# A feed-forward down projection computed with seven half-size products in place of eight

## The reference

```
FFN_HIDDEN = -(-8 * D_MODEL // (3 * 256)) * 256        # 2816

def swiglu(x, w_gate, w_up, w_down):
    return (jax.nn.silu(x @ w_gate) * (x @ w_up)) @ w_down

for l in range(DEPTH):                                  # DEPTH = 2
    mix = hybrid_mixer(x, ...)
    x = layer_norm(ALPHA * x + mix, ln1_g[l], ln1_b[l])
    ffn = swiglu(x, w_ffn_gate[l], w_ffn_up[l], w_ffn_down[l])
    x = layer_norm(ALPHA * x + ffn, ln2_g[l], ln2_b[l])
```

## Time and profile before

| | |
|---|---|
| median of three runs | 2691.89 us (2689.46 to 2693.79) |
| the profiled execution | 2692.8 us, span 2691.0 us |
| PE busy | 2336.5 us, 87% of the span |
| PE weight loads busy (beside PE) | 1520.1 us, 56% |
| DVE busy | 744.4 us, 28% |
| ACT busy | 369.2 us, 14% |
| mean granted clock of TensorE | 0.948 of 2.4 GHz |
| HBM traffic | 241 GB/s over the span |
| the down stage (L2028) in the two layers | 464.05 to 539.78 us and 1006.30 to 1082.03 us |

### The profile page before, as it was taken

One profiled execution on the slowest core, in us unless ns is written; L12 is line 12 of the kernel. 1 busy time (PEld: TensorE's weight loads), 2 busy tenths in 40 slices (PEclk: granted clock), 3 DMA queues, 4 the chain that ended last, 5 costly groups with the idle time before them and its releaser, 6 DMA issues.

```text
span 2691.0 us, 38118 instructions
## 1 busy us (share of the span) xinstructions
PE 2336.5 (87%) x16872; PEld 1520.1 (56%) x16872; DVE 744.4 (28%) x1501; ACT 369.2 (14%) x837; POOL 26.1 (1%) x48
## 2 busy tenths in 40 slices
PE   8999999989999999899989997888799876656564
PEld 6788688477886884445545555554454543323322
DVE  1201472022014730534443221222211441101111
ACT  1211000012210000225433000000102320000000
POOL 0000000000000000000000000000000000000000
PEclk9999999999999999999989999999999988878777
DMA  8443786453436873300044999999910078999996
GB/s 296 153 145 126 242 290 219 146 199 130 152 125 230 286 249 128 135 0 1 1 188 160 423 426 426 426 426 427 381 68 0 0 302 365 427 427 427 428 427 283
DMA packets 165415, 651.84 MB, mean 242 GB/s; under 512 B 7846, under 2 KB 55298, under 8 KB 140290
## 3 DMA queue, kind: packets, MB, share of 16 engines
q1 hardware_dynamic: 161680, 639.66, 61.1%
q0 software_dynamic: 3056, 8.79, 1.0%
q10 hardware_dynamic: 514, 0.94, 0.1%
HBM read 648.27 MB, written 1.08 MB: 241 GB/s over the span
## 4 chain that ended last, share of the span: by engine, by line
PE 55%; issue 28%; DMA 12%; DVE 3%; ACT 1%; DVEq 0%; POOL 0%; SPq 0%; ACTq 0%; POOLq 0%
PE psum L2012 11%; DMA ring<-in_moe_w_up 9%; PE psum L1856 8%; PE psum L1933 6%; PE psum L2028 5%; PE psum L464 4%; PE psum L661 4%; PE psum L1921 3%; PE psum L588 2%; PE psum L456 2%; DMA ring<-in_moe_w_gate 2%; PE psum L678 1%; PE psum L1834 1%; PE psum L1882 1%; DMA ring<-in_moe_w_down 1%
## 5 line engine op out<-in xcount | busy, mean ns | idle before, releaser
L661 PE MATMUL psum<-ring,arena 128*32 128x256 f32 x5952 | 390.9, 419 | 168.7 <-DMA ring<-in_moe_w_up 83.6
L661 PEld LDWEIGHTS psum<-ring,arena 128*32 128x32 f32 x5952 | 212.4, 119 | 343.1 <-issue 143.7
L2012 PE MATMUL psum<-ht,ring 128*128 128x256 f32 x1408 | 311.1, 382 | 2.1 <-ACT ht L2068 2.1
L2012 PEld LDWEIGHTS psum<-ht,ring 128*128 128x128 f32 x1408 | 267.4, 191 | 44.4 <-issue 9.1
L678 PE MATMUL psum<-ring,lnp 128*32 128x256 f32 x3072 | 194.5, 408 | 69.2 <-DMA ring<-in_moe_w_down 63.8
L464 PE MATMUL psum<-ring,ht 128*128 128x512 f32 x448 | 195.0, 594 | 0.0
L678 PEld LDWEIGHTS psum<-ring,lnp 128*32 128x32 f32 x3072 | 104.5, 116 | 158.5 <-DMA ring<-in_moe_w_down 50.6
L1419 DVE TENSOR_TENSOR arena<-psum,gb_moe 32x512 f32<-32x512 f32 (+1 forms) x128 | 70.9, 554 | 373.6 <-PE psum L678 372.3
L1933 PE MATMUL psum<-ht,ring 128*128 128x256 f32 x768 | 166.7, 380 | 0.0
L1933 PEld LDWEIGHTS psum<-ht,ring 128*128 128x128 f32 x768 | 146.3, 190 | 20.3 <-issue 1.0
L2028 PE MATMUL psum<-ring,arena 128*128 128x512 f32 x352 | 151.6, 593 | 1.9 <-DVE arena L2309 1.9
(11 more groups left out here) (350 smaller groups left out, 1933.5 us busy)
## 6 DMA issues: line engine op xcount, KB each, us to landing
ring<-in_moe_w_gate SPq DMA_DIRECT2D x64, 2048.0 KB
ring<-in_moe_w_down SPq DMA_DIRECT2D x64, 2048.0 KB
ring<-in_moe_w_up SPq DMA_DIRECT2D x60, 2048.0 KB
ring<-in_w_in SPq DMA_DIRECT2D x52, 1024.0 KB
ring<-in_ada_w SPq DMA_DIRECT2D x48, 1024.0 KB
ring<-in_w_ffn_gate SPq DMA_DIRECT2D x22, 1024.0 KB
ring<-in_w_ffn_up SPq DMA_DIRECT2D x22, 1024.0 KB
ring<-in_w_ffn_down SPq DMA_DIRECT2D x20, 1024.0 KB
```

Of the source, the lines that this page charges most:

```text
L661: last = mm(bank[32 * j:32 * j + 32, SPLIT * m:SPLIT * m + SPLIT], x_four[:, k, e % 4, SLOTS * m:SLOTS * m + SLOTS], row[:, SPLIT * j:SPLI ...
L2012: last = mm(bank[:, SEQ * u:SEQ * u + SEQ], slot[:, k, SEQ * u + P * h:SEQ * u + P * h + P], xT[:, k, :], start=k == 0, stop=k == KT - 1)
```

## The change

The products of each pair of hidden tiles are regrouped by Strassen's scheme (in the form with seven products). The 256 tokens are cut in two halves of 128, the 1024 columns in two of 512, and the 22 hidden tiles are taken in 11 pairs (`PAIRS`). A quarter of `hid` is then one tile of a pair for one half of the tokens, a quarter of the weights one tile of a pair for one half of the columns. For each pair PE now computes seven products of 128x128 with 128x512, in the order 1, 6, 5, 2, 3, 7, 4 (`SEVEN`), each product number having a bank of its own that accumulates over the 11 pairs.

- **Sums of `hid`** (`turned(a, b)`, DVE): four instructions for the pairs a to b-1. Pairs 0 to 7 are done in one go after p = 8 (four instructions of 128x1024), pair 8 after p = 9, pair 9 after p = 10, pair 10 after the four copies out of the bank `adaGT` (four instructions of 128x128 each). One of the four writes over a quarter of `hid`.
- **Sums of the weights** (`down_sums(d)`, DVE): four instructions for each down panel, 128x1024 for d = 0 to 4 and 128x512 for d = 5. One of them writes over a part of the ring slot, three go to one of three buffers. `down_sums(0)` comes at p = 8, after `turned(0, 8)`; the others come after the gate products. From d = 3 on each waits until PE has finished panel d-3.
- **PE** opens seven banks in place of four before the first product. It goes through panels 0 to 3 pair by pair, and releases each; for panels 4 and 5 (three pairs) it goes product by product, so that the seven banks are finished one after the other, three products apart. Panels 4 and 5 are both released at the end.
- **The tail**: ACT copies the banks of products 1 and 5 to SBUF; DVE combines the seven into the four quarters of `x` (`scaled`, `plus`), normalises t = 0 after product 3, and then adds products 7 and 4 and normalises t = 1. The order of the products in the tail is the same in both layers.
- The tile `gb_moe` of the second network is now a view of a new tile `spare` of the same size, which holds weight sums in the first. `DVE_LAYER`, the number of DVE's counted steps in the loop, goes from 36 to 62.

In the extracts of the instruction order below, `[waits ...]` names the semaphores an instruction waits for, and xN repeats it. L2012 of before is L2022 now, L2309 is L2373, L2319 is L2388, L2257 has become L2400 to L2419, and L2264 to L2274 are L2296 to L2306.

The core of the diff:

```diff
-DVE_LAYER = 36
+DVE_LAYER = 62
+PAIRS = FFN_TILES // 2
+SEVEN = (1, 6, 5, 2, 3, 7, 4)
...
-    layer += [EV] * 5 + [("dn", t, n) for t in range(TT) for n in range(2)]
+    layer += [EV] * 4 + [("dn", c) for c in SEVEN] + [R]
...
-                down = {(t, n): open_bank(pe, "layer", ("dn", t, n), l) for t in range(TT) for n in range(2)}
+                down = {c: open_bank(pe, "layer", ("dn", c), l) for c in SEVEN}
                 wait_emptied(pe, "layer", ("ff", FFN_TILES - 1), l)
-                for f in range(0, FFN_TILES, 4):
-                    slot = panel(l, D)
...
+                    a11, a12, a22 = hid[:, 2 * i, 0:P], hid[:, 2 * i + 1, 0:P], hid[:, 2 * i + 1, P:SEQ]
+                    s1, s2, s4 = (hid_sums[:, m, i, :] for m in range(3))
+                    s3 = hid[:, 2 * i, P:SEQ]
...
+                    return {1: (a11, b11), 2: (a12, b21), 3: (s4, b22), 4: (a22, t4), 5: (s1, t1), 6: (s2, t2),
+                            7: (s3, t3)}[c]
+                slots = [panel(l, D)]
+                pe.wait_ge(hid_sums_ready, l * 4 + 1)
+                for d in range(4):
+                    if d:
+                        slots.append(panel(l, D))
+                    pe.wait_ge(w_sums_ready, l * 6 + (d + 1))
+                    for i in (2 * d, 2 * d + 1):
+                        for c in SEVEN:
+                            left, right = factors(c, i, slots[d], w_sums[d % 3])
+                            last = mm(down[c], left, right, start=i == 0, stop=False)
+                    last.then_inc(pe_done, 1)
+                slots += [panel(l, D), panel(l, D)]
+                pe.wait_ge(hid_sums_ready, l * 4 + 4)
+                pe.wait_ge(w_sums_ready, l * 6 + 6)
+                for c in SEVEN:
+                    for i in range(8, PAIRS):
+                        left, right = factors(c, i, slots[i // 2], w_sums[i // 2 % 3])
+                        last = mm(down[c], left, right, start=False, stop=i == PAIRS - 1)
+                    last.then_inc(pe_done, 1)
...
+                for c, part in ((1, part_1), (5, part_5)):
+                    take(("dn", c), part, part=HALF)
                 root(1, 0)
...
+                def turned(a, b):
+                    for f in range(2 * a, 2 * b):
+                        wait_emptied(dve, "layer", ("ff", f), l)
+                    h4 = hid.rearrange("p (i c) n -> p i c n", c=2)[:, a:b]
+                    a11, a21, a12, a22 = (h4[:, :, c, P * r:P * r + P] for c in range(2) for r in range(2))
+                    s1, s2, s4 = (hid_sums[:, m, a:b, :] for m in range(3))
+                    step(TTo(s1, a21, a22, ALU.add))
+                    step(TTo(s2, s1, a11, ALU.subtract))
+                    TTo(a21, a11, a21, ALU.subtract)
+                    TTo(s4, a12, s2, ALU.subtract).then_inc(hid_sums_ready, 1)
+                def down_sums(d):
+                    n_panel = DOWN_PANEL + d
+                    dve.wait_ge(panel_in[n_panel % RING], l * (32 * LAYER_PANELS // RING) + 32 * (n_panel // RING + 1))
+                    if d >= 3:
+                        dve.wait_ge(pe_done, down_full(d - 3))
...
+                    TTo(t3, b22, b12, ALU.subtract)
+                    step(TTo(b12, b12, b11, ALU.subtract))
+                    step(TTo(t2, b22, b12, ALU.subtract))
+                    TTo(t4, b21, t2, ALU.subtract).then_inc(w_sums_ready, 1)
...
+                    if p == 8:
+                        turned(0, 8)
+                        down_sums(0)
+                    elif p > 8:
+                        turned(p - 1, p)
...
-                for t in range(TT):
-                    add_residual([("dn", t, n) for n in range(2)])
-                    layer_norm(1, t, ln2_loaded, x_ready)
+                turned(PAIRS - 1, PAIRS)
+                dve.wait_ge(pe_done, banks.full("layer", ("ff", FFN_TILES - 1), l))
+                down_sums(1)
+                dve.wait_ge(mods_saved, l * 64 + 64)
+                for d in range(2, 6):
+                    down_sums(d)
...
+                scaled(x00, part_1)
+                plus(part_12, part_1, 6)
+                scaled(x01, part_12)
+                wait_emptied(dve, "layer", ("dn", 5), l)
+                step(TTo(x01, x01, part_5, ALU.add))
+                scaled(x11, part_5)
+                plus(x00, x00, 2)
+                plus(x01, x01, 3)
+                layer_norm(1, 0, ln2_loaded, x_ready)
+                plus(part_all, part_12, 7)
+                scaled(x10, part_all)
+                step(TTo(x11, x11, part_all, ALU.add))
+                plus(x10, x10, 4)
+                layer_norm(1, 1, ln2_loaded, x_ready)
```

More of the change, by code:

```diff
@@ L1588, in program @@
     LAYER_PANELS = banks.stage_panels["layer"][1]
-    ADA_PANEL = 22
+    ADA_PANEL, DOWN_PANEL = 22, 40
     assert LAYER_PANELS % RING == 0
@@ L1610, in program @@
         lnp = sb("lnp", [P, 2, D])
+        spare = sb("spare", [P, 2 * D])
         const = sb("const", [P, 904])
@@ L1643, in program @@
         ada_rows = view(arena[:, 6656:6912], 2, P)
+        hid_sums = view(arena[:, 9984:14208], 3, PAIRS, P)
+        w_sums = [[view(spare[:, 0:1024], 2, HALF), view(spare[:, 1024:2048], 2, HALF), view(arena[:, 14208:15232], 2, HALF)],
+                  [view(ht[:, 1024 * m:1024 * m + 1024], 2, HALF) for m in range(3)],
+                  [view(arena[:, 6912 + 1024 * m:7936 + 1024 * m], 2, HALF) for m in range(3)]]
+        part_1, part_12 = arena[:, 5632:6144], arena[:, 6144:6656]
+        part_5, part_all = ht[:, 3072:3584], ht[:, 3584:4096]
         xT = view(ht[:, 0:2048], KT, SEQ)
@@ L2019, in _, with factors @@
                         transposes("layer", ("adaGT",), [ada_g[:, P * j:P * j + P] for j in range(2)], l)
[L2020 removed]
+                down = {c: open_bank(pe, "layer", ("dn", c), l) for c in SEVEN}
                 wait_emptied(pe, "layer", ("ff", FFN_TILES - 1), l)
[L2022 to L2033 removed]
+                def factors(c, i, slot, sums):
+                    a11, a12, a22 = hid[:, 2 * i, 0:P], hid[:, 2 * i + 1, 0:P], hid[:, 2 * i + 1, P:SEQ]
+                    s1, s2, s4 = (hid_sums[:, m, i, :] for m in range(3))
+                    s3 = hid[:, 2 * i, P:SEQ]
+                    r = i % 2
+                    b11, t1 = slot[:, 2 * r, 0:HALF], slot[:, 2 * r, HALF:D]
+                    b21, b22 = slot[:, 2 * r + 1, 0:HALF], slot[:, 2 * r + 1, HALF:D]
+                    t3, t2, t4 = (e[:, r, :] for e in sums)
+                    return {1: (a11, b11), 2: (a12, b21), 3: (s4, b22), 4: (a22, t4), 5: (s1, t1), 6: (s2, t2),
+                            7: (s3, t3)}[c]
@@ L2303, in ada_sums, with down_full @@
                     V.memset(st[:, 254:255], 0.0).then_inc(ada_ready, 1)
+                def turned(a, b):
[13 more added lines that the diff above has]
+                        dve.wait_ge(pe_done, down_full(d - 3))
+                    n = min(2, PAIRS - 2 * d)
+                    w4 = view(ring[:, n_panel % RING, :], 2, 2, D)[:, 0:n]
+                    b11, b12, b21, b22 = (w4[:, :, c, HALF * m:HALF * m + HALF] for c in range(2) for m in range(2))
+                    t3, t2, t4 = (e[:, 0:n, :] for e in w_sums[d % 3])
+                    TTo(t3, b22, b12, ALU.subtract)
+                    step(TTo(b12, b12, b11, ALU.subtract))
+                    step(TTo(t2, b22, b12, ALU.subtract))
+                    TTo(t4, b21, t2, ALU.subtract).then_inc(w_sums_ready, 1)
+                def down_full(d):
+                    first, per, _ = banks.release[DOWN_PANEL + d]
+                    return l * per + first
                 for p in range(FFN_TILES // 2):
@@ L2321, in _, with scaled, plus @@
                 wait_emptied(dve, "layer", ("adaGT",), l)
-                for t in range(TT):
-                    add_residual([("dn", t, n) for n in range(2)])
-                    layer_norm(1, t, ln2_loaded, x_ready)
+                turned(PAIRS - 1, PAIRS)
[4 more added lines that the diff above has]
+                    down_sums(d)
+                x00, x01, x10, x11 = (x[:, t, HALF * n:HALF * n + HALF] for t in range(TT) for n in range(2))
+                def scaled(xs, part):
+                    step(STT(out=xs, in0=xs, scalar=ALPHA, in1=part, op0=ALU.mult, op1=ALU.add))
+                def plus(out, xs, c):
+                    bank, freed = full_bank(dve, "layer", ("dn", c), l)
+                    TTo(out, xs, bank, ALU.add).then_inc(freed, 1)
+                    wait_emptied(dve, "layer", ("dn", c), l)
+                wait_emptied(dve, "layer", ("dn", 1), l)
+                scaled(x00, part_1)
[12 more added lines that the diff above has]
+                layer_norm(1, 1, ln2_loaded, x_ready)
                 dve.wait_ge(x_ready, 2 * l + 4)
```

12 lines of the change are left out of this document (2 added, 10 removed).

## The result

| | before | after |
|---|---|---|
| median, five runs each, same chip | 2693.79 us (2689.46 to 2698.46) | 2678.79 us (2677.66 to 2681.75) |
| ratio to before | | 0.9944, 95% interval 0.9930 to 0.9959 |
| profiled execution | 2692.8 us, span 2691.0 | 2678.33 us, span 2676.5 |
| DVE busy | 744.4 us | 822.6 us |

The changed kernel is 0.56% faster, by 15.0 us; forecast were 2676.4 us (2672.5 to 2682.8) and a gain of 15.5 us. In 16 and 9 further runs of the kernel before, made beside the experiments on other occasions, the medians were 2691.64 and 2690.33 us, so the gain may be nearer 12.

The account below looks back on a forecast made before the run. The prediction took PE's own rate to bound the down stage. Products -9.47, start +1.68 and tail +0.06 gave -7.73 us per layer, -15.5 for two: 2676.4 us against a median of 2691.89, range 2672.5 to 2682.8.

Parts of the forecast that it names:

- Products: Down stage, per layer: 77 products instead of 88 at an unchanged 0.8606 us each, 9.47 us less, stage 66.26 us.
- the rival of slow products: Down stage: products slow beside a busy DVE, 12% more cancelling the gain, 20% giving 2703 us; chance 0.07.
- The start: Start of the down stage: PE waits for DVE's copies behind four small sums, 1.68 us later per layer, bounds 0.41 to 3.2.
- The clock: Rival: PE's longer wait lowers its clock at the down stage's start, 1.7 us per layer, 2678.1 or 2679.8 us; chance 0.25.
- The prediction's own sign for it: Down stage: a block longer than 66.3 us at a clock under 1.00 would mean the clock gate.
- The tail: DVE's work after the last down product: 0.06 us longer per layer, bounds 1.4 shorter to 2.8 longer.
- The slack of layer 0: After layer 0's down stage: up to 2.84 us of DVE's tail is hidden behind PE's return to the loop start.
- The cover of the weight sums: Down stage: DVE finishes each panel's weight sums before PE wants them, 5.7 us ahead at the thinnest; no cost.
- the loads: Weight panels around the down stage arrive early enough despite changed releases; no cost, or 5.7 us once if cover were gone.
- the sums of hid: Gate stage: about 10 us of DVE sums delay tile 18's gate product from about 443 to 446; no cost.
- The sum: Both layers: -9.47 + 1.68 + 0.06 = -7.73 us each, -15.5 in all, giving 2676.4 us.
- its likeliest case: Whole kernel: the forecast as summed, 2676.4 us, with no clock loss; chance 0.50.

Follow-up runs that it names:

- experiment 1: Changed kernel with DVE's copies out of bank `adaGT` moved to right after the gate products of p = 9; 2671.47 us, ratio to before 0.9925.
- experiment 5: Changed kernel with three throw-away products put into PE's wait ahead of the down stage; 2677.67 us, ratio to before 0.9947.
- experiment 6: Changed kernel without the weight sums of panels 1 to 5, PE reading the ring slots from pair 2 on; 2677.91 us, one execution.
- experiment 3: Kernel before with only the late start: four small DVE sums ahead of the copies, PE waiting for the same banks; 2698.01 us, ratio to before 1.0024.
- experiment 7: Changed kernel with four more chained DVE sums of 128x512 ahead of the tail's second normalisation; 2679.98 us, one execution.
- experiment 4: Changed kernel with product 1 done twice in each pair, so 88 products instead of 77; 2701.93 us, ratio to before 1.0034.
- experiment 8: Changed kernel with early copies, banks opened at first use, no wait for the last gate product, and a shorter DVE tail; 2668.88 us, ratio to before 0.9919.

## Why the prediction was right, and where its sum was not

*Products.* Right to 0.1 us: 77 products at full clock take 66.28 us (experiments 1 and 5), 66.26 had been forecast. That is the rate of before with DVE busy beside it for 32.4 of the 66.28 us, so the rival of slow products is out (experiment 6 agrees).

*The start.* The mechanism was right, DVE's copies behind four small sums hold PE, and the size nearly: 2.01 us from the last gate product to the stage instead of 1.74. Two errors offset each other in part. One small sum took 0.28 to 0.29 us as estimated, but the sums overlap at their ends, and the copies ended 1.38 us after the gate product (469.04 - 467.66), not 1.68. And PE follows the end of the copies by 469.67 - 469.04 = 0.63 us, not 0.06. The likely reason is that further waits stand behind the one on the bank: those for bank 7, the last gate bank, the panel and two counters of sums. The lag is 0.43 in experiments 3 and 5, with three of these, 0.23 in experiment 1 (after the gate product's end at 463.88), with the two counters, and 0.06 before the change, with none. No run changed these waits alone.

*The clock.* The sum put this at nothing. It was a rival at 0.25, priced at 1.7 us a layer, and it came true in both layers: 67.98 and 67.82 us are 1.7 and 1.6 above 66.26. The prediction's own sign for it, a block longer than 66.3 at a clock under 1.00, is what the windows show. The argument against it, that 14 us of dense products come before, was wrong; experiments 3 and 5 show that a wait of 2.7 to 2.9 us behind such products lowers the clock and that filling it keeps it. The Trainium skill, TensorE: Matmul & The Clock Gate, "HAM oscillation — how this bites in real kernels", tells of bursts of matmuls that each start cold after a wait of about 3 to 5 us for a DMA. The waits here are shorter, which the prediction passed over when it applied that section to 2.6 us; the trace shows the same after waits of 2.69 to 2.91 us, and not after the 1.10 us of experiment 1.

*The tail.* Forecast E' + 7.85 for DVE's end, measured 7.60, since the first normalisation ended 0.15 us sooner than counted and the four instructions behind it took 2.98 us, not 3.08; forecast 10.6 and 13.1 for PE's return, measured 10.67 and 12.94. The slack of layer 0 was shown by experiment 7.

*The cover of the weight sums, the loads, the sums of hid.* PE waited for none of them: the blocks have no idle time inside, and the last 64 gate records take 13.98 us as before.

*The sum.* The stage and its start gave 11.8 us, not 2 x (9.47 - 1.68) = 15.6: 3.3 less for the clock and 0.5 for the start. By that alone the time would have been 2691.89 - 11.8 = 2680.1 us, and the gain 11.8. That the measured gain, 15.0, is so near the forecast 15.5 is luck: chance in stretches outside the stage (2.7 us in the two spans) and a kernel before whose five runs beside it lay 2 to 3.5 us above the medians of its later ones. The range held because it had been drawn to take in both falls of the clock. So the forecast was right in its time, its direction and the mechanism of each term that it summed; its likeliest case, the sum without a fall of the clock, isn't the one that came.

## What to carry to other kernels

When work is taken off the engine that sets the pace, look at what the new version waits for before its first product: here one of three more banks to be opened, behind copies that nobody had waited for, cost 3.6 of the 9.5 us per layer, nearly half of it through the clock. Moving those copies to where DVE was idle, and opening each bank at its first use, gave the whole of it back in the traces. And compare two spans stretch by stretch before taking a difference as the change's: stretches outside the changed stage moved by up to 3.7 us here.

## What the runs showed of the hardware

- A wait of 2.69 to 2.91 us of PE right after 14 us of dense fp32 products was followed by matmuls at a granted clock of 0.54 to 0.67 (means over the first 3.3 to 3.4 us), in six of six stages (experiments 3 and 4, the changed kernel), and by blocks 1.6 to 1.7 us longer. In the four stages of experiments 6 and 7, with the same wait, the blocks were 67.76 to 67.99 us, 1.5 to 1.7 us longer too. A wait of 1.10 us was followed by a clock of 1.00, in both stages of experiment 1. After 0.78 to 1.04 us of wait with small transposes before it, the clock fell or stayed as if by chance: the 64 gate records behind it took 15.74 us in 10 of the 20 layers of the ten profiled executions, and 14.05 in the other 10.
- PE's first product came 0.63 us after the release that it had waited for where five further waits stood behind that one, 0.43 with three, 0.23 with two and 0.06 with none. That the number of waits is the cause is a reading of four arrangements.
- 32.4 us of elementwise work on DVE beside 66.28 us of fp32 products, most of it sums that read the same ring slots, didn't lengthen the products by anything that the records show: 0.8608 us each, against 0.8606 with DVE idle.
- After the last matmul of layer 0, PE's return to the start of the loop came with 6.1 to 6.3 us of idle time in every run, whether DVE's tail ended 1.4 us earlier (experiment 8) or 2.9 us later (experiment 7). The cause is open.
